# Absolute value of the stick logits on GpSimd in two passes, and copies and statistics in another order

## What is computed

```python
# softmax head
s = einsum('bqhd,bkhd->bhqk', q, k) * scale          # masked
p = softmax(s);  o = einsum('bhqk,bkhd->bqhd', p, v)
# stick-breaking head
z = einsum('bqhd,bshd->bhqs', qc, kc) * scale
log_beta, log_1m = log_sigmoid(z), where(strict, log_sigmoid(-z), 0)
after = cumsum(log_1m, reverse) - log_1m
a = where(strict, exp(log_beta + after), 0);  oc = einsum('bhqs,bshd->bqhd', a, vc)
o = rms(concat heads) * out_g;  x = x + g2 * (o @ w_out)
```

## Time and profile before

| | us |
|---|---|
| median of 3 runs | 2834.48 |
| range of the runs | 2834.06 to 2837.74 |
| the profiled execution, its own time | 2836.47 |
| its span | 2834.4 |
| mean granted TensorE clock | 0.991 |
| heads' loop of the first layer of the second block | about 2015.6 to 2063.5 |
| heads' loop of the second layer | about 2569.0 to 2621.0 |

### The profile page before, as it was taken

The page is one execution under the profiler, slowest core; times in us unless marked ns, Lnnn a source line. Parts: engine busy times, 40 slices in busy tenths (PEclk is TensorE's granted clock), DMA queues, the critical chain, the costliest instruction groups (busy, mean ns, idle before and its releaser), DMA issues.

```text
span 2834.4 us, 37832 instructions
## 1 busy us (share of the span) xinstructions
PE 2767.2 (98%) x16120; PEld 2426.3 (86%) x16120; DVE 1951.5 (69%) x2187; ACT 1364.6 (48%) x1562; POOL 228.7 (8%) x201
## 2 busy tenths in 40 slices
PE   8999999999999999999999999999999999999999
PEld 6889999998888889999998887888878878788787
DVE  6768876655666678876655667667876676777644
ACT  5444545455445444545455444444644444446433
POOL 0000420000000000420000000003000000030000
PEclk9999999999999999999999999999999999999999
DMA  8655433445776654433446676663266676442554
GB/s 304 258 220 183 153 120 134 171 164 200 267 265 236 257 214 179 149 134 134 162 159 230 254 257 247 253 224 135 103 238 251 246 264 258 183 149 77 197 187 148
DMA packets 82038, 564.42 MB, mean 199 GB/s; under 512 B 9072, under 2 KB 10576, under 8 KB 15952
## 3 DMA queue, kind: packets, MB, share of 16 engines
q1 hardware_dynamic: 66272, 465.47, 44.9%
q0 software_dynamic: 15600, 96.55, 9.1%
HBM read 560.86 MB, written 1.12 MB: 198 GB/s over the span
## 4 chain that ended last, share of the span: by engine, by line
PE 83%; DVE 9%; ACT 3%; POOL 2%; DMA 2%; issue 1%; SPq 0%; POOLq 0%; ACTq 0%; DVEq 0%
PE ps L332 75%; DVE ring_lo L327 3%; ACT w_hi L320 2%; PE ps L899 1%; DMA rows<-mod_rows 1%; POOL qk L2038 1%; PE ps L1287 1%; POOL rope_a L2034 1%; PE ps L530 1%; DVE a_hg L1806 1%; PE ps L1416 0%; PE ps L1442 0%; DVE e L993 0%; DVE e L1786 0%; DVE e L1785 0%
## 5 line engine op out<-in xcount | busy, mean ns | idle before, releaser
L327 DVE TENSOR_TENSOR ring_lo<-ring,w_hi 128x2048 fp32r<-128x2048 f32 x422 | 974.0, 2310 | 478.6 <-ACT w_hi L320 464.2
L320 ACT ACTIVATE w_hi<-ring 128x2048 fp32r<-128x2048 f32 x422 | 806.2, 1910 | 308.5 <-PE ps L332 187.7
L332 PE MATMUL ps<-w_hi,h_hi 128*128 128x512 f32 (+1 forms) x1920 | 731.7, 381 | 17.6 <-DVE h_lo L576 9.2
L332 PE MATMUL ps<-w_hi,h_lo 128*128 128x512 f32 (+1 forms) x1920 | 719.2, 375 | 0.0
L332 PE MATMUL ps<-ring_lo,h_hi 128*128 128x512 f32 (+1 forms) x1920 | 718.7, 374 | 0.0
L332 PEld LDWEIGHTS ps<-w_hi,h_hi 128*128 128x128 f32 x1920 | 365.3, 190 | 84.9 <-DVE ring_lo L327 10.3
L332 PE MATMUL ps<-h_hi,w_hi 128*128 128x256 f32 x1488 | 431.0, 290 | 1.3 <-DVE h_lo L576 1.3
L332 PE MATMUL ps<-h_lo,w_hi 128*128 128x256 f32 x1488 | 422.7, 284 | 0.0
L332 PE MATMUL ps<-h_hi,ring_lo 128*128 128x256 f32 x1488 | 422.6, 284 | 0.0
L332 PEld LDWEIGHTS ps<-w_hi,h_lo 128*128 128x128 f32 x1920 | 364.8, 190 | 65.3
L332 PEld LDWEIGHTS ps<-ring_lo,h_hi 128*128 128x128 f32 x1920 | 365.5, 190 | 61.1 <-issue 1.0
(11 more groups left out here) (359 smaller groups left out, 3430.2 us busy)
## 6 DMA issues: line engine op xcount, KB each, us to landing
ring<-stream SPq DMA_DIRECT2D x438, 1024.0 KB, 4.8
e<-ada POOLq DMA_DIRECT2D x77, 1024.0 KB, 5.9
rows<-mod_rows POOLq DMA_DIRECT2D x18, 512.0 KB, 6.5
rows<-gain_rows POOLq DMA_DIRECT2D x8, 512.0 KB, 4.6
val<-c_row POOLq DMA_DIRECT2D x4, 512.0 KB, 5.2
x<-x_in SPq DMA_DIRECT2D x4, 256.0 KB, 6.7
mem<-mem_t SPq DMA_DIRECT2D x1, 1024.0 KB, 16.1
out_t<-x SPq DMA_DIRECT2D x4, 256.0 KB, 2.1
```

The costliest lines, as they stand in the source:

```text
L320: nc.scalar.activation(hi_of(p), ring[:, p % RING, :], ACT.Copy).then_inc(S.w_hi_ready, 1)
L327: nc.vector.tensor_tensor(lo_of(p), ring[:, p % RING, :], hi_of(p).bitcast(F32), ALU.subtract).then_inc(S.w_lo_ready, 1)
L332: mm = nc.tensor.matmul(out, a, b, start=start and n == 0, stop=stop and n == 2, skip_group_check=group)
```

## The change

Three things change in the loop of each layer. The Abs on ACT (8 per layer) is gone: GpSimd makes -|z| as `max(z, 0) * -2 + z` in two instructions, the first with one tensor input, the second with two, and ACT's Exp follows without the scale of -1. ACT copies the flipped probabilities of heads 4 and 6 at the end of rounds 5 and 7, ahead of `pair_high`, in place of the start of rounds 6 and 8, and `pair_rstd` stands behind `exps`. DVE does `pair_stat` one round later, behind `stick_log`.

```diff
             def softplus(c):
 
-                act.wait_ge(S.zm_ready, nth(S.zm_ready, c + 1))
-                if c >= 2:
-                    act.wait_ge(S.l_ready, nth(S.l_ready, c - 1))
-                zm, sp_ = z_masked[c % 3], st[:, 2 + c % 2, :]
-                chain(nc.scalar.activation(sp_, zm, ACT.Abs))
-                chain(nc.scalar.activation(sp_, sp_, ACT.Exp, scale=-1.0))
+                act.wait_ge(S.abs_ready, nth(S.abs_ready, c + 1))
+                sp_ = st[:, 2 + c % 2, :]
+                chain(nc.scalar.activation(sp_, sp_, ACT.Exp))
                 nc.scalar.activation(sp_, sp_, ACT.Ln, bias=one[:]).then_inc(S.soft_ready, 1)
...
             for i in range(HEADS_2 + 4):
-                if 0 <= i - 2 < HEADS_2:
+                paired = i >= 5 and i % 2 == 1
+                if 0 <= i - 2 < HEADS_2 and (paired or i < 6):
                     flipped(i - 2)
-                if i >= 5 and i % 2 == 1:
-                    pair_rstd((i - 5) // 2)
                 if i < HEADS_2:
                     exps(i)
+                if paired:
+                    pair_rstd((i - 5) // 2)
                 if 0 <= i - 2 < HEADS_2:
                     sticked(i - 2)
...
                 if i < HEADS_2:
                     softplus(i)
-                if i >= 5 and i % 2 == 1:
+                if paired and i - 1 < HEADS_2:
+                    flipped(i - 1)
+                if paired:
                     pair_high((i - 5) // 2)
...
                 if 0 <= i - 1 < HEADS_2:
                     stick_log(i - 1)
+                if i >= 5 and i % 2 == 1:
+                    pair_stat((i - 5) // 2)
                 if 0 <= i - 2 < HEADS_2:
                     stick_arg(i - 2)
...
                 if 5 <= i and i % 2 == 1:
                     pair_scaled((i - 5) // 2)
-                if 4 <= i < HEADS_2 + 4 and i % 2 == 0:
-                    pair_stat((i - 4) // 2)
...
             send_mods(pool, l, 5, 9, sent + 2, sent + 2)
+            for c in range(HEADS_2):
+                pool.wait_ge(S.zm_ready, nth(S.zm_ready, c + 1))
+                if c >= 2:
+                    pool.wait_ge(S.l_ready, nth(S.l_ready, c - 1))
+                nc.gpsimd.tensor_scalar(st[:, 2 + c % 2, :], z_masked[c % 3], 0.0, -2.0, ALU.max,
+                                        ALU.mult).then_inc(S.twice_ready, 1)
+                pool.wait_ge(S.twice_ready, nth(S.twice_ready, c + 1))
+                nc.gpsimd.tensor_tensor(st[:, 2 + c % 2, :], st[:, 2 + c % 2, :], z_masked[c % 3],
+                                        ALU.add).then_inc(S.abs_ready, 1)
             pool.wait_ge(S.o_done, nth(S.o_done, HEADS_2))
```

More of the change, by code:

```diff
@@ L140 @@
     pv_done=8, ada_done=22, head_sq=4, head_ss=4, head_var=4, head_rs=4,
-    head_ready=4, ki_ready=1, logit_done=6, relu_ready=6, relu_used=6, z_done=8, zm_ready=8, soft_ready=8,
+    head_ready=4, ki_ready=1, logit_done=6, relu_ready=6, relu_used=6, z_done=8, zm_ready=8, twice_ready=8, abs_ready=8, soft_ready=8,
     l_ready=8, cum_done=8, arg_ready=8, a_ready=8, wi_ready=2,
@@ L282, in program @@
             "ada_done", "silu_row", "head_sq", "head_ss", "head_var", "head_rs", "head_ready", "ki_ready",
-            "logit_done", "relu_ready", "relu_used", "z_done", "zm_ready", "soft_ready",
+            "logit_done", "relu_ready", "relu_used", "z_done", "zm_ready", "twice_ready", "abs_ready", "soft_ready",
             "l_ready", "log_done", "h_scaled", "h_hi_ready", "down_done", "mem_loaded", "c_loaded", "con_loaded", "ones_loaded", "con_next",
```

## The result

The changed kernel takes 2845.12 us (median of 8 runs, 2842.03 to 2846.69), the kernel before, run beside it, 2836.51 (8 runs, 2834.06 to 2840.08). The ratio is 1.0035 [1.0026, 1.0044]: slower by 0.35%. The span of the profiled execution is 2843.8 us, 9.4 more than before.

A forecast was written before the change was run, and what follows sets the result against it. PE was taken as the bound, other engines mattering only where PE stands still. Passes +4.2 and order -1.9 per loop gave +4.6 for two, clock +1.6: +6, so 2840.5 us; range 2830.5 to 2850, the forecast's own 2836 to 2845.

The forecast's parts named there:

- the case that had 0.50: Main forecast: POOL held by DVE, low clock at the start of at least one loop, +2 to +10 us.
- the prediction's own last sentence: Wrong if POOL's first pass takes under 1 us beside a split, over 1.2 alone, or middle rounds are POOL's or DVE's.
- late low stretch: Low clock late in the second loop, worth 4.1 us; half was counted as going with the copies' waits, -2.1 us.
- Step 1: Head 0 at the loop's start: DVE's split holds POOL's first pass, so ACT's Exp starts 2.9 us late.
- Step 2: Head 1: its Abs is saved on ACT; PE's wait for head 0's copy grows from 1.67 to about 4.1 us.
- Step 3: Head 2: round 2's split gets in between POOL's two passes; head 1's copy is 4.2 us late.
- Step 4: Heads 3 to 7: `stick_log` and POOL hold each other 0.3 to 0.5 us a head, paid by the 0.54 us Abs.
- Step 5: PE's clock: low stretch behind the 4.1 us wait, less half the second loop's old one; +1.6 us, range 0 to +7.
- adding up: Rival, chance 0.18: PE's low clock delays DVE and so the next heads, POOL's first pass longer; +15 us, 2849.
- POOL not held: Rival, chance 0.08: the passes run beside DVE's splits; -2.0 us per loop, 2830.5, or 2826.4 without the second loop's low clock.
- the early gain is cancelled: Rival, chance 0.10: the order gives 2.8 us, the first pass takes 0.33 us; +0.1 per loop, 2834.7 us.
- The clock stays up: Rival, chance 0.14: the 4.1 us wait brings no low stretch; +4.6 or +0.5 us, 2835 to 2839.

The follow-up runs named there:

- order_only: Changed kernel with only the new order of copies and statistics; Abs back on ACT, no POOL passes: 2829.42 us, 0.9983 of the kernel before.
- clock_both: Changed kernel plus unused matmuls in PE's waits, four ahead of `flip(1)` and two ahead of `sums(6)`: 2835.03 us, 1.0000 of the kernel before.
- clock_kept: Changed kernel plus four unused matmuls of 512 columns in PE's wait ahead of `flip(1)`: 2843.49 us, 1.0028 of the kernel before.
- pool_from_3: Changed kernel with POOL's passes for heads 3 to 7 only, ACT doing the Abs of heads 0 to 2: 2836.61 us, 1.0009 of the kernel before.
- order_clock: New order alone, Abs on ACT, plus one unused matmul ahead of `sums(6)`: 2827.78 us, 0.9972 of the kernel before.
- pool_first_3: Changed kernel with POOL's passes for heads 0 to 2 only, ACT doing the Abs of heads 3 to 7: 2845.78 us, 1.0039 of the kernel before.
- split_first: Changed kernel with DVE's split of round 0 issued ahead of the loop: 2840.93 us, 1.0022 of the kernel before.
- one_op: Changed kernel with one operation, not two, in POOL's first pass, output not the right one: 2845.81 us, 1.0040 of the kernel before.
- split_clock: Changed kernel with round 0's split ahead of the loop and two unused matmuls each ahead of `flip(1)` and `sums(6)`: 2832.47 us, 0.9993 of the kernel before.

## Why the prediction was right and where it missed

The time lies within the range, and the change of +8.6 us (medians) within the +2 to +10 of the case that had 0.50. The forecast of 2840.5 is 4.6 us too low; 2.0 of these are the kernel before, which stands at 2836.5 and not at 2834.5, the rest is the change, +8.6 for +6. Its mechanism, POOL held by DVE and a low clock behind PE's wait, is the one that the runs show. Two sizes were off, the first pass and the late low stretch. By the prediction's own last sentence it is wrong on one point: POOL's first pass takes over 1.2 us alone.

| per loop | predicted | measured |
|---|---|---|
| new order | -1.9 | -1.9 (order_only) |
| passes, full clock | +4.2 | +5.0 (clock_both less order_only) |
| sum, full clock | +2.3 | +3.1 |
| early low stretch | +2.3, at 0.8 | +2.3 (clock_kept), in both loops |
| late low stretch | second loop, half of 4.1 left | +3.0, in both loops (5.3 less 2.3) |

**Step 1** had Exp(0) 2.9 us late; it is 3.7 (7.40 behind the first scores, 3.71 before). The hold came as forecast: 1.9 us. What failed is the length of the first pass, taken as 0.65 us between bounds of 0.33 and 1.0; it takes 1.49 alone. That it "reads once and writes once" was the wrong measure. With one operation it takes 1.17, so even with one operation it is above the upper bound, and the second costs 0.33 more. The estimate from the Trainium skill, "GPSIMD Engine Reference", section "4.1 Engine selection", of 0.32 us plus the start, is further off still, and the trace disagrees with it: the one-input pass is longer than the two-input one of 1.0 us. The second pass was forecast at 1.0 and took 1.01.

**Step 2** had PE's wait at 4.1 us; it is 4.79. The surplus is again the first pass.

**Step 3** had +4.2 at Exp(2) and at head 1's copy; both are +4.7 (18.77 for 14.05, and 19.85 for 15.12, behind the first scores). Its detail was partly wrong, and two errors cancelled. The split of round 2 was to wait for POOL's first pass and slip in between the passes. In fact it started at 2031.05, in the middle of the first pass (2030.29 to 2032.02), and ran its usual 2.28 us. The first pass took 1.73 because `stick_log(1)` had begun 0.17 ahead of it: it ended 1.35 behind `stick_log`'s end at 2030.67, as head 0's ended 1.35 behind its split. The second pass then was held for 1.1 us, from 2032.10 to 2034.19, and took 2.09, not over 3. So the longer first pass added about what the shorter hold took away. With a first pass of 1.0 the bounds had +4.1 per loop; with 1.49 it is +3.1, so they made its weight too great.

A one-input pass in flight does hold DVE, but only at its start. `stick_log` at 2053.59, 0.30 us behind the pass of 2053.29, takes 0.62 for 0.55. At 2035.43, 0.43 us behind the pass of 2035.00, it takes 0.56. An estimate from these: DVE is held until about 0.4 us behind the pass's start. The Trainium skill has in "SBUF — State Buffer", section "Who interferes with whom", that the second to start blocks fully. The trace agrees for a POOL pass that starts behind a split (1.88 us held), and disagrees where a split starts 0.76 us behind a one-input POOL pass (2.28 us, not held).

**Step 4** had heads 3 to 7 pay for themselves. The middle rounds stayed PE's: `flip(3)` and `flip(4)` are 3.55 us apart (2042.13 and 2045.68), with no wait at either. Nearly right at full clock: behind `turn_back(0)` 0.5 of the 5.0 us arises. They are not free, though: in pool_from_3 the passes of heads 3 to 5 cost 1.1 us up to `turn_back(0)`. Among its costs was one that I had not listed: the second pass holds DVE's small sums of eight columns, 0.71 and 0.97 us in place of 0.16 (the one at 2045.15 ends at 2045.86, with the pass that runs from 2044.84 to 2045.84).

**Step 5**, the clock, was the larger miss. The early stretch came in both loops. That it cost the 2.3 us forecast is luck: they were worked out for a length of 8 us, and by the same formula the 10.2 that it lasts would be 3.4.

The late stretch was to be half gone, since it "comes after the waits for the two copies, which go". That reading was wrong. The rows of the second loop before show it from about 2604, right behind the waits of 1.08 and 0.99 ahead of `flip(6)` and `sums(6)`, which the prediction did not list, and the second copy's wait, at 2609.16, stands inside it. Neither of those two waits goes; after, they are 0.78 and 1.90. Filling the one ahead of `sums(6)` takes the stretch away, by clock_both and order_clock. The late stretch now comes in both loops. pool_first_3 has it in both too, without passes in heads 3 to 7 and with waits of 1.32 and 1.03, as order_only's, where one loop of the two has it. So it needs neither the passes beside it nor the wait of 1.90, and what decides in which loop it comes is not shown. That only waits longer than those at the loops' starts bring the low clock did not hold in the trace of before either: its low stretch at 2276, shown above, begins behind a wait of 1.36 us:

```profile
2276.16 0.47 PE L332 MATMUL ps<-w_hi,h_hi 128*128 128x512 f32 x1 [1.36 <-DVE h_lo L576]
```

Sum: 2 x 3.1 + 2 x 5.3 - 4.1 (the old late stretch) = +12.7 in the loops, -3.4 outside them, +9.3 of the span's 9.4. The forecast for the loops was +6.2, half of that. That the time came out within 5 us of the forecast is owed to the 3.4 us outside the loops, on which nothing in it counted: that is luck.

Of the rivals, "adding up" (+15, 2849) came near to the loops' 12.8, though not by its mechanism: the late stretch follows the late waits and no delay runs from the early one to it, since clock_kept removes the first, in its first loop, and has the second in full. "POOL not held" and "the early gain is cancelled" are refuted by the first pass: 3.37 us beside the split and 1.49 alone. "The clock stays up" gave 2835 to 2839, 0.5 to 4.6 over the kernel before; clock_both, which makes it so, has 1.0000 [0.9991, 1.0009], within a margin of 2.5 us.

What stays open: why the places outside the loops, unchanged, show 10 us less of low clock, and why of two loops with the same waits one has the late stretch and the other not. Both are seen, also between other kernels here, and no run aims at them.

## What to carry to other kernels

Before work goes from a busy engine to an idle one, ask whether it lies on the chain and what it costs there. Here 0.54 us of ACT became two passes of 2.6 us in a row, in front of the heads whose copies PE waits for, to relieve an engine that was not the bound. Look up what runs beside it: in these traces a DVE instruction with two SBUF inputs that started first held POOL's pass until its own end. And count the clock with every new wait on PE: here it cost 5.3 us per loop, as much as the passes themselves (5.0), and a few matmuls without use in the waits gave it back.

## What the runs showed of the hardware that was not expected

- A POOL pass with one input over 128x384 elements takes 1.49 us with two operations (split_first, head 0) and 1.17 with one (one_op); the pass with two inputs takes 1.00.
- The hold is not the same both ways. A one-input POOL pass waits for the end of a DVE instruction with two SBUF inputs that started first, and ends 1.35 us behind it. The other way round, a DVE split that started 0.76 us behind such a pass took its 2.28 us, and `stick_log` 0.30 us behind one lost 0.07. The two-input pass held DVE instructions of 8 columns until its own end, for 0.55 and 0.81 us.
- The clock fell to 0.50 also behind short waits with work between them: 1.08 and 0.99 us in the second loop before, 0.78 and 1.90 after. It did not in the first loop before, with the same waits. Added matmuls of 1.0 to 3.6 us in the waits kept it at 1.00 through both loops in clock_both, split_clock and order_clock.
